# Filling TensorE's waits inside the norms with multiplications of constants, and taking the early column sums into the last tile's product

## The reference: what is computed

```python
mu = jnp.mean(xf, -1, keepdims=True)
var = jnp.mean(jnp.square(xf - mu), -1, keepdims=True)
y = (xf - mu) * lax.rsqrt(var + LN_EPS)
```

## Time and profile before

| | us |
|---|---|
| three runs, median | 3772.85 |
| three runs, lowest and highest | 3770.77, 3780.21 |
| the profiled execution, its own time | 3767.59 |
| its span, first to last instruction | 3766.3 |
| TensorE busy in the span | 3578.6 (95%) |
| VectorE, ScalarE, GpSimd busy | 1759.2, 1234.8, 507.3 |

### The profile page before, as it was taken

One profiled execution on the slowest core, in us unless ns is written; L12 is line 12 of the kernel. 1 busy time (PEld: TensorE's weight loads), 2 busy tenths in 40 slices (PEclk: granted clock), 3 DMA queues, 4 the chain that ended last, 5 costly groups with the idle time before them and its releaser, 6 DMA issues.

```text
span 3766.3 us, 40780 instructions
## 1 busy us (share of the span) xinstructions
PE 3578.6 (95%) x16716; PEld 2898.0 (77%) x16716; DVE 1759.2 (47%) x3072; ACT 1234.8 (33%) x1670; POOL 507.3 (13%) x433
## 2 busy tenths in 40 slices
PE   8999999899998999999899989988999998999999
PEld 7888767678886888767688876746878887787887
DVE  5544553555444544444533234685543333564332
ACT  2222362332223222462332223234442223343222
POOL 1010121110011010121110011111121111202111
PEclk9999899999998999999899998988999999999999
DMA  6443222134432443211122221100212222222222
GB/s 257 166 148 145 102 86 81 56 123 149 164 135 101 155 158 131 83 46 45 50 105 90 100 73 58 66 12 34 90 62 96 101 101 72 99 75 82 101 92 76
DMA packets 52604, 373.40 MB, mean 99 GB/s; under 512 B 5825, under 2 KB 5953, under 8 KB 9538
## 3 DMA queue, kind: packets, MB, share of 16 engines
q1 hardware_dynamic: 52418, 370.79, 27.3%
HBM read 368.67 MB, written 2.10 MB: 98 GB/s over the span
## 4 chain that ended last, share of the span: by engine, by line
PE 86%; DVE 7%; ACT 4%; issue 2%; POOL 1%; DMA 0%; ACTq 0%; DVEq 0%; SPq 0%; POOLq 0%
PE ps L1215 85%; DVE s_wl L1844 1%; ACT s_wh L1537 1%; DVE s_hl L1838 1%; PE ps L1235 0%; DVE s_xr L1932 0%; ACT L1642 0%; DVE s_tmp L2064 0%; DVE s_hh L1938 0%; ACT s_tmp L1673 0%; DVE s_tmp L2054 0%; POOL s_tmp L2340 0%; ACT s_hh L1537 0%; POOL s_hl L2316 0%; DVE s_sm L2062 0%
## 5 line engine op out<-in xcount | busy, mean ns | idle before, releaser
L1215 PE MATMUL ps<-s_hh,s_wh 128*128 128x512 f32 (+1 forms) x2840 | 1138.7, 401 | 59.8 <-DVE s_hl L1838 32.7
L1215 PE MATMUL ps<-s_hl,s_wh 128*128 128x512 f32 (+1 forms) x2840 | 1120.5, 395 | 0.0
L1215 PE MATMUL ps<-s_hh,s_wl 128*128 128x512 f32 (+1 forms) x2840 | 1119.8, 394 | 0.0
L1844 DVE TENSOR_TENSOR s_wl<-s_stage,s_wh 128x2048 fp32r<-128x2048 f32 (+1 forms) x277 | 628.5, 2269 | 721.7 <-ACT s_wh L1537 721.5
L1537 ACT ACTIVATE s_wh<-s_stage 128x2048 fp32r<-128x2048 f32 (+1 forms) x277 | 519.8, 1877 | 732.6 <-PE ps L1215 621.8
L1215 PEld LDWEIGHTS ps<-s_hh,s_wh 128*128 128x128 f32 (+1 forms) x2840 | 541.8, 191 | 203.5 <-issue 68.9
L1215 PEld LDWEIGHTS ps<-s_hh,s_wl 128*128 128x128 f32 (+1 forms) x2840 | 541.1, 191 | 117.5 <-issue 0.2
L1215 PEld LDWEIGHTS ps<-s_hl,s_wh 128*128 128x128 f32 (+1 forms) x2840 | 542.6, 191 | 113.1 <-issue 2.4
L1215 PE MATMUL ps<-s_ah,s_wh 128*128 128x512 f32 x1216 | 474.4, 390 | 0.0
L1215 PE MATMUL ps<-s_ah,s_wl 128*128 128x512 f32 x1216 | 473.2, 389 | 0.0
L1215 PE MATMUL ps<-s_al,s_wh 128*128 128x512 f32 x1216 | 473.1, 389 | 0.0
(11 more groups left out here) (414 smaller groups left out, 3285.9 us busy)
## 6 DMA issues: line engine op xcount, KB each, us to landing
s_stage<-in_w_ada SPq DMA_DIRECT2D x64, 1024.0 KB, 4.8
s_stage<-in_ffn_w_gate SPq DMA_DIRECT2D x44, 1024.0 KB, 4.8
s_stage<-in_ffn_w_up SPq DMA_DIRECT2D x44, 1024.0 KB, 4.8
s_stage<-in_ffn_down SPq DMA_DIRECT2D x32, 1024.0 KB, 4.8
s_stage<-in_w_up SPq DMA_DIRECT2D x32, 1024.0 KB, 4.8
s_stage<-in_down_m SPq DMA_DIRECT2D x32, 1024.0 KB, 4.7
s_stage<-in_w_in SPq DMA_DIRECT2D x24, 1024.0 KB, 4.8
s_stage<-in_ffn_down SPq DMA_DIRECT2D x16, 768.0 KB, 4.2
```

The lines of the kernel that those rows point to most:

```text
L1215: return pe.matmul(out, lhs, rhs, start=start, stop=stop, skip_group_check=True)
L1844: dve.tensor_tensor(m.WL[:, ws, 0:n], m.STAGE[:, j % NS, 0:n], m.WH[:, ws, 0:n].bitcast(F32), ALU.subtract).then_inc(*e.up("dve_w", "w.lo" ...
```

## The change

A new TensorE helper multiplies the identity by 256 columns of constants, `n` times, into a bank whose content nobody reads. It is put into seven places: behind the making of the first h (8 times, as a step `pace` with a bank of its own), in `ln_a` ahead of the sums of squares (7), in `ln_b` and `ln_last` ahead of the spread (5), behind `ln_b` (5), in `rms_a` where nothing was summed before (2; only g_mix of layer 0), in `rms_b` ahead of the spread (5) and behind it (3), the last two not in the g_xattn norms.

`total` is now called for each tile but the last two as soon as the next tile has been updated, and for tile 6 within the product of tile 7, at three quarters of its rows. There TensorE also makes the sums that were left until then: for a column-mean norm the buffer and tile 6 into `mean` (`ln_most`), for a scaling norm two of the three `stat`s (`rms_most`). Only tile 7's is left behind the product. With `within`, the call takes the place of the tick at that row.

```diff
+    def keep(self, n):
+        b = self.banks.take()
+        i = self.new()
+        self.add("pace", i, b, n)
+        self.banks.free(b, ("pace", i))
-    def feat(self, ch, kt, nc, t, x, ver, n=S, m=P, off=None):
+    def feat(self, ch, kt, nc, t, x, ver, n=S, m=P, off=None, within=None):
...
-        for k in range(0, kt, 4):
-            self.add("mm", self.pid, ch, kt, nc, t * P if off is None else off, m, n, b, x, ver, k, min(k + 4, kt))
-            if k + 4 <= kt:
-                self.tick()
+        ends = sorted({kt, *range(4, kt, 4), *([kt * 3 // 4] if within else [])})
+        for k, end in zip([0] + ends, ends):
+            self.add("mm", self.pid, ch, kt, nc, t * P if off is None else off, m, n, b, x, ver, k, end)
+            if within and end == kt * 3 // 4:
+                within()
+            elif end % 4 == 0:
+                self.tick()
...
+    def early(self, of, total, state):
+        sid, acc = total
+        def within():
+            self.total(of, *total, [NT - 2])
+            if of == "ln":
+                state.append(self.banks.take())
+                self.add("ln_most", sid, acc[0], self.xv[NT - 2], state[0])
+            elif of == "rms":
+                state.append(self.held.take())
+                self.add("rms_most", sid, acc[:2], state[0])
+        return within
...
         self.add("mod_first", s, self.hv, self.to_h())
+        self.keep(8)
...
             self.add("ln_b", sid, y, var, rs, s, self.hfree, self.hv, self.to_h(), low)
+            self.keep(5)
...
-        self.add("rms_b", rid, name, l, y, b, qs, list(self.xv), self.hfree, self.hv, low)
+        self.add("rms_b", rid, name, l, y, b, qs, list(self.xv), self.hfree, self.hv, low, 0 if meanwhile else 5)
+        if not meanwhile:
+            self.keep(3)
...
-                    b, pid = self.feat(ch, G, 256, t, "a%d" % a, av)
+                    n = 2 * c + t
+                    b, pid = self.feat(ch, G, 256, t, "a%d" % a, av,
+                                       within=self.early(mean, total, state) if summed and n == NT - 1 else None)
...
+                    if summed and 0 < n < NT - 1:
+                        self.total(mean, *total, [n - 1])
...
+    def keep(b, n):
+        for _ in range(n):
+            ins = mul(b[:, 0:256], m.ident, m.CC[:, 0:256])
+        return ins
+    def pace(i, b, n):
+        e.wait_ge(("cc",), b.after)
+        keep(m.bank(b), n).then_inc(*e.up("pe_pace", "pace", i))
...
-    def ln_a(l, idx, sid, acc, nxt, xv, s, mean, sq, var):
+    def ln_most(sid, acc, v, mean):
         ones = m.col1024.to_broadcast([P, P])
         e.wait_ge(("xs", sid, NT - 3), mean.after)
         mul(m.bank(mean), ones, m.tmp(acc), True, False)
-        for n in (NT - 2, NT - 1):
-            e.wait_ge(xe(n, xv[n]))
-            ins = mul(m.bank(mean), ones, m.XR[:, n, :], False, n == NT - 1)
-        ins.then_inc(*e.up("pe_norm", "ln.mean", sid))
+        e.wait_ge(xe(NT - 2, v))
+        mul(m.bank(mean), ones, m.XR[:, NT - 2, :], False, False).then_inc(*e.up("pe_norm", "ln.most", sid))
+    def ln_a(l, idx, sid, nxt, xv, s, mean, sq, var):
+        e.wait_ge(xe(NT - 1, xv[NT - 1]))
+        mul(m.bank(mean), m.col1024.to_broadcast([P, P]), m.XR[:, NT - 1, :], False, True).then_inc(
+            *e.up("pe_norm", "ln.mean", sid))
         e.wait_ge(var.after)
+        keep(m.bank(var), 7)
...
     def ln_b(sid, y, var, rs, s, hfree, hv, qs, low_of):
-        e.wait_ge(("rs", sid), rs.after)
+        e.wait_ge(rs.after)
+        keep(m.bank(rs), 5)
+        e.wait_ge(("rs", sid))
         spread(m.bank(rs), m.y(y), range(4)).then_inc(*e.up("pe_norm", "ln.rs", sid))
...
+    def rms_most(sid, acc, st):
+        e.wait_ge(st.after)
+        for i, event in enumerate((("xs", sid, NT - 3), ("xq", sid, NT - 2))):
+            e.wait_ge(event)
+            ins = stat(m.bank(st), 0, 1, m.tmp(acc[i]), m.col1024, i == 0, False)
+        ins.then_inc(*e.up("pe_norm", "rms.most", sid))
```

More of the change, by code:

```diff
@@ L319, in layer_norm @@
     def layer_norm(self, l, idx, total, nxt):
-        sid, acc = total
+        sid, acc, mean = total
         if nxt:
@@ L323, in layer_norm @@
             self.modded(nxt[0], nxt[1])
-        s, mean = self.small.take(), self.banks.take()
+        s = self.small.take()
         self.tmp.free(acc[0], ("ln.mean", sid))
@@ L359, in layer_norm @@
         self.small.free(s, ("ln.sub", sid, NT - 1))
-        return [(sq[n], ("ll.fold", sid, n)) for n in (3, 5, 7)]
+        return [(sq[n], ("ll.fold", sid, n)) for n in (3, 5, 7)], None
     def rms_norm(self, name, l, total, meanwhile=None):
         rid, low = self.new(), None
-        st, y = self.held.take(), self.yr.take()
-        self.add("rms_a", rid, total, st, y)
-        for q, _ in total:
+        part, st = total
+        first, y = not st, self.yr.take()
+        st = st or self.held.take()
+        self.add("rms_a", rid, part, first, st, y)
+        for q, _ in part:
             self.tmp.free(q, ("rms.st", rid))
@@ L416, in ffn @@
                 self.hfree = ("proj", pid)
-            done, s = [], None
+            summed = gi == len(groups) - 1 and mean
             for c in range(4):
@@ L420, in ffn, with summed @@
                 for t in range(2):
-                    b, pid = self.feat(ch, G, 256, t, "a%d" % a, av)
+                    n = 2 * c + t
+                    b, pid = self.feat(ch, G, 256, t, "a%d" % a, av,
+                                       within=self.early(mean, total, state) if summed and n == NT - 1 else None)
                     if gate and not gate[-1]:
                         gate[-1] = self.gate(l, gate[0], 0.5)
-                    self.upd(2 * c + t, b, pid, gate[-1] if gate else None)
-                    done.append(2 * c + t)
+                    self.upd(n, b, pid, gate[-1] if gate else None)
+                    if summed and 0 < n < NT - 1:
+                        self.total(mean, *total, [n - 1])
                 self.release(ch, ("proj", pid))
                 afree[a] = ("proj", pid)
-                if gi == len(groups) - 1 and mean:
-                    self.total(mean, *total, done[:-2] if c < 3 else done)
-                    done = done[-2:] if c < 3 else []
         if gate:
             self.small.free(gate[-1][0], ("x", NT - 1, self.xv[NT - 1]))
-        return total if mean != "rms" else self.squares(*total)
+        return self.summed(mean, total, state)
+    def summed(self, of, total, state):
+        if of == "ln":
+            return total + (state[0],)
+        if of == "rms":
+            sid, acc = total
+            self.total(of, *total, [NT - 1])
+            for q in acc[:2]:
+                self.tmp.free(q, ("rms.most", sid))
+            return [(acc[2], ("xq", sid, NT - 1))], state[0]
+        return None
     def project_out(self, name, idx0, kt, nc, x, ver, gate, mean, order=None):
-        total, done, per = (self.new(), []), [], nc // P
+        total, state, per = (self.new(), []), [], nc // P
         for c in range(NT // per):
@@ L439, in project_out @@
             tiles = (self.feat2(ch, kt, x, ver, True, order=order) if per == 2 and c == 0 else
-                     (self.feat(ch, kt, nc, t, x, ver) for t in range(per)))
+                     (self.feat(ch, kt, nc, t, x, ver,
+                                within=self.early(mean, total, state) if per * c + t == NT - 1 else None)
+                      for t in range(per)))
             for t, (b, pid) in enumerate(tiles):
-                self.upd(per * c + t, b, pid, gate)
-                done.append(per * c + t)
+                n = per * c + t
+                self.upd(n, b, pid, gate)
+                if 0 < n < NT - 1:
+                    self.total(mean, *total, [n - 1])
             self.release(ch, ("proj", pid))
-            last = c == NT // per - 1
-            self.total(mean, *total, done if last else done[:-2])
-            done = done[-2:]
         self.hfree = ("proj", pid)
-        return total if mean != "rms" else self.squares(*total)
+        return self.summed(mean, total, state)
     def tick(self):
```

41 lines of the change are left out of this document (23 added, 18 removed).

## The result

| | before | after |
|---|---|---|
| median of the timed runs, us | 3775.21 (20 runs) | 3784.44 (20 runs) |
| lowest and highest | 3770.77, 3780.21 | 3772.26, 3792.09 |
| profiled execution, span | 3766.3 | 3788.0 |
| a second profiled execution, span | 3775.7 | 3785.9 |

The ratio is 1.0023, 95% interval 1.0015 to 1.0032: 9.2 us slower, less than the 0.3% that I call no change, but 0.4 us over the upper end of the forecast range. The 20 executions of the changed kernel spread over 20 us, those of before over 9, and the time goes with the granted clock: 0.976 and 0.975 in the two fastest (3772.26 and 3775.24), 0.969 to 0.970 in the six slowest.

A forecast was written before the change was run, and what follows sets the result against it. TensorE was taken as busy 95% of the span, leaving only norm idle stretches and the clock to win. Terms 0 + 2.0 - 0.3 - 1.3 - 0.6 = -0.2 us on 3767.59, median 5.3 above: 3772.6; range 3750 to 3784.

The forecast's parts named there:

- the clock: Column-mean norms: clock falls in or just behind the sums of squares, returns under the constants; half-clock stretches 3 to 7 us.
- The rule of the Trainium skill: Rival, all norms: without long idle gaps the clock holds through the sums; -19.0 us, 3753.9; chance 0.23.
- The third rival: Constants don't count for the clock: it falls as now, constants run at half clock; about +41 us, 3814; chance 0.06.
- the moved sums: Column-mean norms: early sums lose the cover of the last tile's update and lengthen the product; subtraction +1.1 us in each.
- The failed step: Six column-mean norms: two places of the clock's fall held equally likely; 0.0 per norm, 0 for six, bounds -5.4 and +5.4.
- the first case: Column-mean norm: clock falls behind the sums of squares, spread follows at full clock; scaling starts 0.9 us sooner.
- the second case: Column-mean norm: clock falls in the middle of the sums of squares; scaling starts 0.9 us later.
- Scaling norms: Three open scaling norms: moved sums and late constants against a shorter product; g_mlp +1.0 each, g_mix of layer 1 -0.3.
- g_mix 0: Norm behind 6.43 us of idle: constants 1.9 late, spread may win 1.0, product 2.1; -1.3 us.
- The start: Eight constants before the first product: 2.0 us too many at half clock, but bring the clock back; -0.6, at worst +2.0.
- Together 0: Other edits (earlier squares and additions, one tick less, bank for the constants): no net cost, 0 us.
- The second rival: Constants ahead of the spread overrun and the spread stays at half clock; +19.1 us, 3792; chance 0.11.

The follow-up runs named there:

- the best version: Kernel before plus the constants, 3 instead of 5 ahead of the spreads, no sum moved: 3763.08 us, ratio 0.9965; in a second session 3756.99 us, 0.9949.

## Why the prediction was wrong, point by point

**Right: the clock.** It fell in or behind the sums of squares in every column-mean norm and came back under the constants; the stretches are 3.4 to 10.3 us (I had said 3 to 7), the mean clock 0.971 (0.975). The rule of the Trainium skill that I had set against it (TensorE: Matmul & The Clock Gate, "Why this matters for your kernels": no long idle gaps between bursts) would have held the clock, 3753.9; TensorE is idle for 0.84, 0.38 and 0.19 us between U and the spread in the norm above, and the clock fell all the same, so the trace disagrees with that rule here. It is so in all twelve norms of the two executions: no idle stretch from the product's end to the spread is longer than 0.84 us. The third rival (constants don't count) fell too: the clock is back before the product, and the product runs at full clock.

**Right: what counts is the first scaling.** From there to the 48th multiplication it is 17.2 us before and after in four of the first five column-mean norms, though the product starts at half clock before and at full after (the third has 15.3 and 16.0 before and 15.2 after). A clock that comes back sooner wins nothing there.

**Right: the moved sums,** by their first part: predicted +1.1 at the subtraction, measured 1.74 - 0.60 = 1.14. But the price at the first scaling is 1.4 alone and 1.8 beside the constants, since the 0.60 is lost again on the way.

**The failed step: "Nothing in the rows makes one likelier than the other: 0.0 per norm".** I had two cases, the fall behind the sums (-0.9) and in the middle of them (+0.9), and took their mean. Of twelve norms in two executions one came near the first case (first scaling at U + 14.88, with the 1.74 that is -0.5), and eleven lie 0.5 to 2.1 above the mean before. The mean is +0.74, near the second case. By its terms, against the mean of my cases: root 12.5 us behind A instead of 12.25, spread 1.75 late instead of 1.45, 1.5 to the scaling instead of 1.1, since in some norms the spread still runs at the low clock (0.9 in all; the mean before lies 0.16 above the one norm that I had read). What would have spoken for the second case is the change's own shift: the moved sums push the whole chain behind U 1.74 later against the product's stream and bring only 0.60 back, while the fall hardly moves with it (U + 8.3 instead of 9.6 in the means of two executions each; 9.6 is the version with the sums in their old place; without any constants U + 4.7 with the sums moved, 6.4 before). More of the sums so run at the low clock, and the 0.60 is spent. Six norms: +4.5 instead of 0.

**Scaling norms:** +1.9 measured for +1.7. (By my own terms a held clock comes to -1.4, not -1.3, and g_mix 0 to -1.2; neither matters to the sum.) For g_mlp 0 each term stands: root +1.76 (1.7), constants 1.41 late (1.9), product 2.07 shorter (2.1); net 0.0 instead of +1.0. **g_mix 0** was mis-sized: -1.3 forecast, +1.0 measured. I had credited it with the product's 2.1, but its product takes 15.8 us from the first scaling for 15.9 before, at either clock, and the five constants are 1.89 late. **The start**: -0.6 forecast, -1.0 measured; the eight constants make the first product no later (41.96 for 42.01 in the earlier trace rows), and its second record lasts 0.40, at full clock:

```profile
36.88 5.44 PE L1253 MATMUL ps<-s_cc 128*128 128x256 f32 x16
41.96 0.59 PE L1253 MATMUL ps<-s_hh,s_wh 128*128 128x512 f32 x1
42.39 0.40 PE L1253 MATMUL ps<-s_hl,s_wh 128*128 128x512 f32 x1
```

**A term at nothing: the parts between the norms.** The forecast came to 3772.6 and the runs to 3784.44, 11.8 more. The kernel before has a median of 3774.1 to 3776.1 where three runs had given 3772.85: 2.4 of it, by the runs beside the changed kernel. The norms give +6.4 instead of -0.2. Some 3 are left for the parts between the norms; the two profiled pairs, whose spans differ by 16.0, have 9.6 there, of which 8.8 repeat between g_mix 0 and g_mlp 0. My "Together 0" weighed the other edits and not the clock in these parts, and named no bound for it. The range was missed by 0.4 us, less than any one of these terms.

**The second rival (keeps overrun)** was nearer than I gave it (0.11): its place and mechanism are what the run with two constants shows, 7.1 us of the changed kernel. Its price was not: 1.9 late was in my forecast already, and it had the low clock through the spread each time, which came in some.

## What to carry to other kernels

A filler for a wait is sized by the wait at the low clock, not at the full one: three multiplications of 0.85 us end 0.2 behind a root of 2.39, five 1.9. With two for five the changed kernel goes from +0.23% to break-even; with three for five and the sums left alone it goes from break-even to 0.35% faster. Work that is moved off the end of a stage must have been on the path there: the sums of tile 6 had lain under the last update, and in the product they cost their full 1.74 us each time. When a sum of terms rests on where the clock falls, work out what the change does to that place; the mean of two cases is not a neutral choice. And what is won in the edited places is not yet the kernel's: here 12 us won in the norms by the constants alone came with 12 lost between them, so the parts that an edit leaves alone need a term and a bound too.

## What the runs showed of the hardware that I had not expected

- Two norms with the same TensorE records at the same offsets (within 0.02 us, from 32 us ahead of U to the fall) had the clock at 1.00 throughout and at 0.50 for 10.3 us. So whether the clock falls wasn't settled by TensorE's work there alone.
- TensorE streaming without a gap can stand at 0.50: 10.30 of 10.30 us busy behind 1866.05. What had gone before were sums of one column with constants between them.
- Sums of one column take about twice as long at half clock as at full, though they have only one column each: 24 in 5.28 us where the clock stood at 0.50 and in 2.73 at full. The 4.42 us of the changed kernel's norm above are a mixture: the first 1.0 us of them still ran at full clock.
- The clock in the parts between the norms differs by 20 us at 0.50 in one mixer (37.5 and 17.1) between two executions of the same kernel, and moved its span by 6.3 us; another stretch repeated to 0.3 us in the kernels before and after and differed by 10.6 between them, but took 487.2 and 483.5 in two executions of the best version.
